# Fifteen up blocks instead of thirteen, in runs of seven, six and two, with one low part moved on the VectorE queue

## The reference, cut to what matters

```
h  = rmsnorm(x, g_ffn)
up = h @ w_up                        # (512, 1024) @ (1024, 5632)
a, u = up[..., :2816], up[..., 2816:]
a = causal_depthwise_conv(a, conv_w, conv_b)      # 3 taps along the tokens
x = x + (gelu(a) * u) @ w_down
```

## Time and profile before

| | |
|---|---|
| runs | 873.79, 873.88 (the profiled one), 874.05, 874.26 us, the median of the three unprofiled ones 874.05 |
| span in the profile | 872.1 us |
| PE busy | 866.0 us (99%) |
| DVE busy | 665.2 us (76%) |
| ACT busy | 490.6 us (56%) |
| granted TensorE clock | 1.0 over the whole span |

### The profile page before, as it was taken

How to read it: one execution, slowest core, us unless ns; L and a number is a source line. 1 busy time by engine, 2 the same in 40 slices (tenths; PEclk the granted TensorE clock), 3 DMA queues, 4 the chain that set the end, 5 groups by cost and what they waited for, 6 DMA issues and landing times.

```text
span 872.1 us, 13414 instructions
## 1 busy us (share of the span) xinstructions
PE 866.0 (99%) x4996; PEld 764.4 (88%) x4996; DVE 665.2 (76%) x949; ACT 490.6 (56%) x737; POOL 46.6 (5%) x67
## 2 busy tenths in 40 slices
PE   9999999999999999999999999999999999999998
PEld 7798898888888889999888999999999888998887
DVE  7897796796796896775568888888888967557744
ACT  7875766766865744443367556665554443434531
POOL 1200000000000000000001212121210000000000
PEclk9999999999999999999999999999999999999999
DMA  7233233233233133225434576666653323322241
GB/s 280 85 115 116 73 104 115 72 100 116 70 99 96 61 109 109 89 95 180 146 97 111 170 202 167 175 177 173 184 143 121 109 91 115 98 86 89 91 151 67
DMA packets 35669, 105.64 MB, mean 121 GB/s; under 512 B 4993, under 2 KB 6289, under 8 KB 35489
## 3 DMA queue, kind: packets, MB, share of 16 engines
q1 hardware_dynamic: 28496, 87.57, 30.8%
q0 software_dynamic: 6048, 13.70, 7.2%
q10 hardware_dynamic: 1072, 3.67, 1.2%
HBM read 97.85 MB, written 2.10 MB: 115 GB/s over the span
## 4 chain that ended last, share of the span: by engine, by line
PE 98%; DVE 1%; ACT 0%; issue 0%; DVEq 0%; ACTq 0%
PE dense L650 21%; PE dense L651 21%; PE dense L652 21%; PE aty L651 5%; PE aty L652 5%; PE aty L650 5%; PE z L650 5%; PE z L652 5%; PE z L651 5%; PE z L724 2%; PE aty L757 1%; DVE fs L1930 1%; PE aty L834 1%; PE aty L774 1%; PE aty L772 1%; DVE w_lo L1930 0%
## 5 line engine op out<-in xcount | busy, mean ns | idle before, releaser
L650 PE MATMUL dense<-hi,w_hi 128*128 128x512 f32 (+1 forms) x752 | 291.2, 387 | 0.0
L651 PE MATMUL dense<-lo,w_hi 128*128 128x512 f32 (+1 forms) x752 | 288.5, 384 | 0.0
L652 PE MATMUL dense<-hi,w_lo 128*128 128x512 f32 (+1 forms) x752 | 288.2, 383 | 0.0
L1930 DVE TENSOR_TENSOR w_lo<-w_f,w_hi 128x1024 fp32r<-128x1024 f32 (+3 forms) x139 | 155.5, 1121 | 45.9 <-ACT w_hi L1157 36.8
L652 PEld LDWEIGHTS dense<-hi,w_lo 128*128 128x128 f32 x752 | 141.4, 188 | 28.1
L650 PEld LDWEIGHTS dense<-hi,w_hi 128*128 128x128 f32 x752 | 141.5, 188 | 27.1 <-issue 0.8
L651 PEld LDWEIGHTS dense<-lo,w_hi 128*128 128x128 f32 x752 | 141.6, 188 | 25.7 <-issue 0.2
L1157 ACT CAST w_hi<-w_f 128x1024 fp32r<-128x1024 f32 (+3 forms) x92 | 87.9, 956 | 46.2 <-PE dense L652 36.4
L1930 DVE TENSOR_TENSOR fs<-fs 128x512 f32<-128x512 f32 (+3 forms) x152 | 108.0, 717 | 5.6
L650 PE MATMUL z<-hi,w_hi 128*128 128x256 f32 x340 | 96.4, 284 | 1.2 <-DVE w_lo L1930 1.2
L652 PE MATMUL z<-hi,w_lo 128*128 128x256 f32 x340 | 96.2, 283 | 0.0
(11 more groups left out here) (191 smaller groups left out, 1240.6 us busy)
## 6 DMA issues: line engine op xcount, KB each, us to landing
w_f<-in_w_in SPq DMA_DIRECT2D x52, 512.0 KB, 3.4
w_f<-in_w_up SPq DMA_DIRECT2D x44, 512.0 KB, 4.2
fs<-in_w_up POOLq DMA_DIRECT2D x38, 256.0 KB, 4.0
w_f<-in_w_down SPq DMA_DIRECT2D x16, 512.0 KB, 3.5
w_f<-in_w_b SPq DMA_DIRECT2D x8, 512.0 KB, 3.3
w_f<-in_w_out SPq DMA_DIRECT2D x8, 512.0 KB, 3.2
w_f<-in_w_pg SPq DMA_DIRECT2D x8, 512.0 KB, 3.3
cst<-in_w_up POOLq DMA_DIRECT2D x14, 256.0 KB, 4.6
```

The lines of the kernel that those rows point to most:

```text
L650: mm(out, w1, x1, start=start, stop=False, skip_group_check=skip)
L651: mm(out, w1, x0, start=False, stop=False, skip_group_check=skip)
L652: return mm(out, w0, x1, start=False, stop=stop, skip_group_check=skip)
L1930: return nc.vector.tensor_tensor(out, a, b, op).then_inc(done, 1)
```

## The change

```
-UP_BLOCKS = (2, 3, 5, 6, 7, 9, 10, 11, 13, 14, 15, 17, 18)
+UP_BLOCKS = (2, 3, 4, 5, 6, 7, 8, 10, 11, 12, 13, 14, 15, 17, 18)
```

Tiles 4, 8 and 12 become blocks, tile 9 becomes plain. The runs are now 2 to 8, 10 to 15, and 17 and 18. In TensorE's list, `up_between` (the plain tile behind a run) takes its waits by the parity of the run's length:

```
 def up_between(f):
-    pe.wait_ge(s_read, read(UP0 + 2 * f - (5 if run_before(f) == 2 else 4)))
+    pe.wait_ge(s_read, read(UP0 + 2 * f - (4 if run_before(f) % 2 else 5)))
+    if run_before(f) % 2 == 0 and (UP0 + 2 * f) % 3:
+        pe.wait_ge(s_half11, UP_BLOCKS.index(f - 1) + 1)
```

In VectorE's list, from the third block of a run on, the low part of the first chunk is taken out of the block's own `up_second` and put at the end of that of the block before, ahead of the gating:

```
 def up_second(n):
     up_sum(n, 2)
     up_sum(n, 4)
-    low_first_weights(c)
+    if not behind_block(n - 1):
+        low_first_weights(c)
     if not over_forms(n - 1):
         low_g(f - 2)
...
     up_left(n)
     if f + 1 in UP_BLOCKS:
+        low_first_weights(c + 2)
         value(f - 1)
         return
```

## The result

| | median us | lowest to highest |
|---|---|---|
| before | 873.95 | 873.79 to 874.26 |
| changed | 886.69 | 885.83 to 888.53 |

The changed kernel is slower: ratio 1.0149, 95% interval 1.0136 to 1.0161. The forecast was 884.7, in a range of 880 to 889. Its four runs are 2.7 us apart, where those of before differ by 0.5.

A forecast was written before the change was run, and what follows sets the result against it. PE, busy 99% of the span, was taken as the bound, with VectorE and ScalarE setting the pace in long runs. Span 872.1 - 3.6 + 8.2 + 6.2 = 882.9 us, plus 1.8 around it, gives 884.7; range 880 to 889.

The forecast's parts named there:

- What goes: TensorE, up stage: two plain tiles becoming blocks save 1.66 us, three product 1 stalls save 1.95; together 3.6 us.
- What is late next: VectorE, from a run's third block: the moved low part leaves a 1.53 us wait for ScalarE's high part of g.
- The turn: VectorE and ScalarE, block to block in long runs: 12.01 us against PE's 10.08, so 1.93 us lost a block.
- Where PE feels it: Product 5 waits for ScalarE's snapshot 1, product 3 for form 2's low part; block ends no earlier than low g + 9.7.
- Losses of 8.2 and 6.25: Microseconds PE loses to the slower turn in the run of seven blocks and in the run of six.
- No loss behind the runs: Plain tiles, the next run's lead, and the pair 17 and 18 add nothing after a long run.
- Transfers: GpSimd's sets of four per block: later sets have room at 12.01 us; nothing taken, 0 to 2 us kept for range.
- a wait of VectorE for a transfer: Sign of a wrong forecast: in long runs, VectorE waiting for a transfer at the place of its wait for g.
- PE stays the bound: Rival: the turn is at or under 10.08 us, so PE gets faster, 870.3 us; chance 0.06.
- the gap closes by itself: Rival: turn of 10.48 us, third block's low g at its start (T3) + 0.84; no change, 874.1 us; chance 0.06.
- Transfers set the pace: Rival: GpSimd's sets make the turn 13.97 us, 13.7 us more, 898.4 us; chance 0.04.
- The clock did not fall: Rival judged: PE's pauses drop the clock to 1.2 GHz, 57 us more, about 942 us; chance 0.01.

The follow-up runs named there:

- e4: The kernel before, with its thirteen blocks, plus only the moved low part of the weights: 873.81 us, ratio 0.9998.
- e7: The kernel before with thirteen blocks, the moved low part, and g's high part first on ScalarE: 872.01 us, ratio 0.9979.
- e2: The changed kernel, with GpSimd issuing form 3's first transfer right behind form 1's first, not after its landing: 885.04 us, ratio 1.0127.
- e5_both: The changed kernel, with g's high part first on ScalarE and form 3's first transfer issued right behind form 1's on GpSimd: 871.17 us, ratio 0.9971.
- e3: The changed kernel, with the low part of a block's first chunk back behind the sums of forms 2 and 4: 884.46 us, ratio 1.0123.

## Why the prediction was right

*What goes.* Two more blocks and the three stalls, 3.6 us. Right: e4 and the profile after show third blocks starting 10.08 us behind the second; e7 brought 1.93 of the stalls' 1.95 us, in its profile, when nothing took their place.

*What is late next.* The low part fills the gelu's hole and opens one ahead of low g. Right, with its size: a wait of 1.45 us was measured, 1.53 forecast (from start to start it is 1.53). The table isolates it. With ScalarE's old order the move costs 5.7 us, with g first it brings 5.3.

*The turn.* 12.01 forecast, 11.99 to 12.00 measured in the run of six, and in the run of seven once transfers are out of the way (e2). The distance of 12.07 that stood beside it as a check agreed by luck: as the prediction says, it was another sum, with the gelu's wait in place of most of the wait for g. The closed hole gives 10.46, the bound of 10.48.

*Where PE feels it.* Product 3 and product 5, and 9.8 us from low g to the start of the next block (614.16 to 623.95) where I had 9.7. Losses of 8.2 and 6.25, measured 8.2 and 6.3 in e2. No loss behind the runs: right, 10.90 us for the plain tile.

*Transfers.* The term that was mis-sized. I took nothing, spoke of 0 to 2 us and put up to 1 us into the range. In the profiled execution they cost 3.1 us in the run of seven; in the medians 1.65 (886.69 against 885.04). I had worked out the first transfers of the run, for which the margin held, and said that later sets have room. They had not: a set took 12.2 to 13.0 us, and a set can't start before the last is done. That the sets are this long because SyncE's weight loads run beside them is likely by the times in the trace, but no run isolates it; what e2 shows is that they are not late any more once the first transfer of form 3 does not wait for the landing of form 1's. The prediction had named a wait of VectorE for a transfer as a sign that it was wrong. That sign came, in the run of seven (0.43 to 1.04 us): there the sets, and not VectorE and ScalarE alone, gave the distance of the blocks, and the total stayed in the range because the excess over 12.0 us was small.

*Rivals.* That PE stays the bound, or that the gap closes by itself, is out. The price of the second was wrong, though: it kept low g of the third block at T3 + 0.84 with the wait of 1.53 gone from the turn, but then this low g comes 1.5 us earlier too. e5_both, which has that turn, loses 0.6 us and not 3.7, and took 871.17 and not 874.1. Transfers set the pace partly, only in one run. The clock did not fall in the changed kernel, whose stops are split in two of 1.7 and 1.1 us at most; it did in e3.

## What to carry to other kernels

Where an in-order queue has holes, an instruction moved into one leaves another where it was: read what the instruction behind it waits for before counting the move as free. Then compute the turn from one tile to the next for each engine pair, since a run of three may live on slack that a run of seven has not. A wait on an engine with a quarter of its time idle can be most of the loss; here one line on ScalarE was worth 10.7 us.

## What the runs showed of the hardware

- TensorE's clock fell from its upper level of 2.4 to 1.2 GHz in e3, behind stops of 2.47 and 2.11 us from start to start, each a block after an earlier stop (1.61 and 0.67 us). Some sixteen matmuls each time started 0.21 us apart instead of 0.12, which is 1.5 us. Stops of 1.84 and 1.20 us in one block of the changed kernel left it at 1.00. The Trainium skill (TensorE: Matmul & The Clock Gate, section "Why this matters for your kernels") names longer idle gaps than these as what to avoid; here the clock fell behind these two, and the measurement decides.
- A transfer of 256 KB from GpSimd's queue took from 2.8 to 8.0 us from issue to landing in the profile of the changed kernel; what made the difference was not isolated. Two issued 0.6 us apart and then awaited in order took most of the variation out of the time: 885.83 to 888.53 became 884.88 to 885.10, four runs each.
